# Two mixers and two expert layers on one core: decay gates moved to ScalarE, gate features projected earlier, output weights converted further ahead, and the first expert query put ahead of two weight conversions

## The chip, the cores and the metric

One core of a Trainium2 chip runs the whole program. The metric is device time in microseconds (us) of one execution. The engines are TensorE (PE, its weight loads PEld), VectorE (DVE), ScalarE (ACT), GpSimd (POOL) and the queue engine SyncE (SP).

## The reference

`x` is 256 tokens by 1024 features, all in fp32. Two blocks follow one another:

```
x = x + mixer1(rmsnorm(x)) ; x = x + peer(rmsnorm(x)) ; x = rmsnorm(x)      # first block
x = x + mixer2(rmsnorm(x)) ; x = x + peer(rmsnorm(x)) ; x = rmsnorm(x)      # second block
```

`peer` picks, for each token and each of 8 heads, 16 of 16,384 single-neuron experts from two sets of 128 keys, gathers their two rows of 1024 numbers, and sums gate * gelu(u.x) * v.

`mixer2` projects its input to ten groups of 1024 features. Three go through a causal convolution of width 4 and silu and become q, k, v of a gated delta rule in chunks of 64: q and k are brought to unit length, a triangular system (I + tril(k k^T beta decay)) is solved per chunk, with decay = exp(G_i - G_j) below the diagonal and G the running sum of the log gates g. The output is normed and gated by silu(ag). A second recurrence takes f (forget gates, `bf`), q (`bq`), input (`bi`) and an output gate (`bg`). The two results go through `w_branch_a` and `w_branch_b`, are weighted with sigmoid(ga) and sigmoid(gb), summed, and go through `w_out`.

## The kernel before, in words

All activations stay on chip. The program has five instruction streams, each written by a function of its own (`tensor_program`, `scalar_program`, `vector_program`, `gpsimd_program`, `sync_program`), and every order is written out by hand. Semaphores join them: `full(key)` says that TensorE has filled a PSUM bank, `taken(key)` that the bank was read and is free. TensorE takes the eight banks in turn.

**Weights.** `plan` lists all weight blocks in the order of use. SyncE loads each block (512 KB) into one of four slots of `ring`. Most blocks are cut into two pieces. A piece is converted into `parts` (6 places): ScalarE writes the high part (`hi`, a rounding copy, line 903) and VectorE or GpSimd the low part (`lo` = raw - hi, lines 1283 and 2134). `by_pool(p)` says which of the two does piece p. TensorE then makes three matrix products for one exact one (`mm3`, lines 357 to 359). An item of four pieces gives 256 output columns and costs 48 matmuls. ScalarE's conversion of piece p waits until TensorE has used piece p - 6. `ahead(n)` in each stream means: let the conversions go n pieces further, to six beyond the present position, but never beyond `cap[0]`. `w_branch_a` (`wa`) is used raw from the ring, in whole blocks; `cap` holds conversions back behind its blocks (`behind_wa`).

**Mixer 2** (about 842 to 1349 us of the span), stages in order of TensorE:
1. 12 convolution items (`conv`). VectorE runs the taps and silu of each; ScalarE its tanh. Between them `delta_gates` makes the gates: VectorE fills `TG` (16 slices, triu scaled by g, line 1796), TensorE sums them over rows into four banks `D` (line 662), VectorE takes the gaps to G and clips them into `DT` (line 1802), ScalarE takes exp, VectorE masks with `triu` (`decay`, line 1807).
2. `ag` item 0, transposes of q, k, v to tokens (`qk`, line 677), `ag` items 1 to 3. Meanwhile VectorE makes the unit lengths (squares, sums, root on ScalarE, products: lines 1858 to 1873; call it the unit chain). Then q, k, v are transposed back (`back`, line 688).
3. Products `L` and `Q` (line 705) times `DT`, and a block inverse in 24 steps (`inverse_y`, line 732, `inverse_xt`, line 741, `inverse_turned`, line 697).
4. The state products, then the second recurrence with 7 levels (`level_ex`, `level_exp`, `level_qk`, `level_taken`; TensorE line 819), one item between two levels.
5. Tail: `features("wb")`, `ya` 2 and 3, `yb` 0 to 3, `w_out2`, residual `x3`.

The items `bf`, `bq`, `bi`, `ya` 0 and 1, `bg`, `ga`, `gb`, `ya` 2 and 3 (`fillers`) are put between the other stages one by one with `item()`, in the same order in every stream.

**Expert layers** (`experts(e, ...)`, e = 1 and 2): GpSimd loads `keys` (line 2146), TensorE makes query item 0, `keyed(0)` scores it against the keys (line 581), ScalarE moves the scores to `S` (line 1034), VectorE `chosen(0)` picks the first 16 experts of each token (lines 1556 to 1606), and GpSimd starts 256 indirect loads of 128 rows of 8 KB each (line 2156, ten landing places). For each loaded set VectorE makes the dot product (line 1630), ScalarE the weight (line 1053), TensorE the sum (line 604). The choices of the later heads and query items 3 to 7 are fitted in between.

The arena's regions are reused by hand: `BF` lies over the first columns of `CT`, which holds q, k, v by feature until the state products.

Of the kernel before, what the change touches and what calls it, by code (L numbers as in the profile page):

```python
# [25 lines left out]
NLEV = 7  # L26

# [51 lines left out]
def build(nc, d, out):  # L79
    ctx = ExitStack()  # L80
    with ctx:
# [142 lines left out]
        BF = region(2048, 2048, c=8)  # L224
# [11 lines left out]
        SS = region(26624, 1024, h=8)  # L236
        WT = region(27648, 1024, h=8)
# [3 lines left out]
        bkf, bff, bqf = region(10240, 2048), region(2048, 2048), region(4096, 2048)  # L241
        BB, BFs, bb = spare[:, :].rearrange("p (s n) -> p s n", s=16), region(2048, 2048, s=16), spare[:, :]
# [88 lines left out]
        def tensor_program(pq, pe):  # L331
# [307 lines left out]
            def delta_gates():  # L639
# [16 lines left out]
                yield  # L656
                yield
                yield
                for q in range(4):
                    o = bank(("D", q))  # L660
                    pq.wait_ge(*on(("TG", 15)))
                    pe.matmul(o[:, :], ones, TG[:, 4 * q:4 * q + 4, :], start=True, stop=True).then_inc(*full(("D", q)))
                    yield
# [45 lines left out]
            def items():  # L709
                for name, i in fillers:  # L710
                    if name in ("bf", "bq"):
                        yield by_feature, (name, i), "w_in2", "n1"
                    elif name == "ya":
                        yield by_token_whole, (name, i), "wa", "oT", oT
                    else:
                        yield by_token, (name, i), "w_in2", "n1"
            left = items()

            def item():
                kind, *a = next(left)  # L720
                kind(*a)

# [170 lines left out]
        def scalar_program(aq, ac):  # L893
# [229 lines left out]
            def delta_gates():  # L1123
# [1185 lines left out]
```

## Time and profile before

| | |
|---|---|
| median of 3 runs | 2039.79 us (2035.16 to 2040.49) |
| profiled execution | 2036.71 us, span 2034.9 us |
| mean granted TensorE clock | 0.973 |
| PE / PEld / DVE / ACT / POOL busy | 84% / 51% / 66% / 45% / 41% |
| HBM read | 635.07 MB, 313 GB/s over the span |

The profile shows one execution. "Idle before, with a releaser" is the time in which an engine waited, and the instruction of another engine or DMA whose end let it go on. The busy share of TensorE is modelled from pipelined instructions, so it says little alone; its waits say more.

### The profile page before, as it was taken

The numbers are of one execution on the slowest core, as the hardware profiler recorded it, in microseconds if no ns is written. First come the engines' busy times: TensorE is split into PE (matmuls) and PEld (weight loads), VectorE is DVE, ScalarE is ACT, GpSimd is POOL, SyncE is SP. The second block draws the span as 40 slices with busy tenths as digits, with TensorE's granted clock in tenths as the row PEclk, the third lists the DMA queues.
The fourth block names the chain that finished last, engine by engine and source line by source line (L and its number), as shares of the span: only waits on it lengthen the run. The fifth ranks groups of instructions, "written<-read, shape, count | busy, mean of one in ns | idle before, by whom it ended". The sixth has DMA issues, their size and how long they took to land.

```text
span 2034.9 us, 22626 instructions
## 1 busy us (share of the span) xinstructions
PE 1702.4 (84%) x7622; PEld 1047.5 (51%) x7622; DVE 1336.4 (66%) x2922; ACT 913.9 (45%) x2366; POOL 839.4 (41%) x762
## 2 busy tenths in 40 slices
PE   8986889877887778789799989977899787777887
PEld 7985444422322222579799989973444222222222
DVE  4666776766776664499646773547776677667644
ACT  5554545444544443445324344454444444444443
POOL 4325333333333333367525465544333333333331
PEclk9998999999999999999899999989999999999999
DMA  7446999999999999543213333559999999999996
GB/s 247 129 129 267 420 421 421 422 421 421 422 421 421 421 421 422 216 135 125 73 53 101 100 112 114 167 169 421 421 421 421 421 422 422 421 422 421 421 422 286
DMA packets 102052, 637.60 MB, mean 313 GB/s; under 512 B 11264, under 2 KB 12544, under 8 KB 36144
## 3 DMA queue, kind: packets, MB, share of 16 engines
q0 software_dynamic: 75216, 543.73, 64.3%
q1 hardware_dynamic: 26720, 92.43, 14.1%
q8 instruction: 60, 0.98, 0.2%
q14 instruction: 56, 0.46, 0.1%
HBM read 635.07 MB, written 1.05 MB: 313 GB/s over the span
## 4 chain that ended last, share of the span: by engine, by line
PE 38%; DMA 34%; DVE 16%; ACT 8%; issue 3%; POOL 0%; SPq 0%; DVEq 0%; ACTq 0%
DMA arena<-in_uv,arena 29%; PE pb L604 19%; DMA spare<-in_uv,arena 4%; PE pb L357 4%; PE pb L358 4%; PE pb L359 4%; ACT arena L1053 3%; DVE arena L1630 3%; PE pb L430 1%; PE pb L741 1%; ACT parts L903 1%; PE pb L732 1%; DVE arena L1821 1%; DVE parts L1283 1%; DMA arena<-in_sk 1%
## 5 line engine op out<-in xcount | busy, mean ns | idle before, releaser
L604 PE MATMUL pb<-arena 128*128 128x512 f32 x1848 | 910.2, 622 | 223.9 <-ACT arena L1053 222.0
L1630 DVE SCALAR_TENSOR_TENSOR arena<-arena,pb 128x1024 f32<-128x1024 f32 x462 | 563.3, 1219 | 375.2 <-DMA arena<-in_uv,arena 375.2
L2156 POOL DMA_INDIRECT arena<-in_uv,arena x462 | 438.3, 949 | 734.0 <-PE pb L604 681.9
L604 PEld LDWEIGHTS pb<-arena 128*128 128x128 f32 x1848 | 321.8, 192 | 779.3 <-ACT arena L1053 511.3
L2134 POOL TENSOR_TENSOR parts<-ring,parts 128x512 fp32r<-128x512 f32 x228 | 340.1, 1510 | 346.3 <-ACT parts L903 344.0
L1045 ACT ACTIVATE arena<-arena 128x1 f32<-128x1 f32 x512 | 103.3, 202 | 621.7 <-DVE arena L1630 567.3
L903 ACT ACTIVATE parts<-ring 128x512 fp32r<-128x512 f32 x328 | 197.8, 627 | 198.8 <-PE pb L359 183.2
L1053 ACT ACTIVATE arena<-cst,arena 128x128 f32<-128x128 f32 x512 | 205.5, 401 | 48.7 <-ACT arena L1048 1.1
L357 PE MATMUL pb<-xl,parts 128*128 128x256 f32 x704 | 221.6, 315 | 4.1 <-DVE xl L1315 2.6
L358 PE MATMUL pb<-xh,parts 128*128 128x256 f32 x704 | 201.3, 286 | 0.0
L359 PE MATMUL pb<-xh,parts 128*128 128x256 f32 x704 | 201.1, 286 | 0.0
L357 PE MATMUL pb<-parts,xh 128*128 128x256 f32 x608 | 176.7, 291 | 14.2 <-DVE parts L1283 9.6
L358 PE MATMUL pb<-parts,xl 128*128 128x256 f32 x608 | 174.2, 287 | 0.0
L359 PE MATMUL pb<-parts,xh 128*128 128x256 f32 x608 | 174.1, 286 | 0.0
L1048 ACT ACTIVATE arena<-arena 128x1 f32<-128x1 f32 x512 | 150.8, 294 | 19.3 <-ACT arena L1045 0.4
L1283 DVE TENSOR_TENSOR parts<-ring,parts 128x512 fp32r<-128x512 f32 x100 | 78.2, 791 | 104.3 <-ACT parts L903 104.1
L357 PEld LDWEIGHTS pb<-xl,parts 128*128 128x128 f32 x704 | 137.2, 195 | 16.4 <-issue 13.8
L358 PEld LDWEIGHTS pb<-xh,parts 128*128 128x128 f32 x704 | 137.3, 195 | 10.8 <-issue 10.8
L359 PEld LDWEIGHTS pb<-xh,parts 128*128 128x128 f32 x704 | 136.9, 195 | 0.0
L357 PEld LDWEIGHTS pb<-parts,xh 128*128 128x128 f32 x608 | 118.9, 196 | 15.1 <-DVE parts L1283 10.0
L358 PEld LDWEIGHTS pb<-parts,xl 128*128 128x128 f32 x608 | 119.0, 196 | 0.0
L604 PE MATMUL pb<-spare,arena 128*128 128x512 f32 x200 | 99.6, 621 | 23.2 <-ACT arena L1053 23.1
(297 smaller groups left out, 1779.2 us busy)
## 6 DMA issues: line engine op xcount, KB each, us to landing
ring<-in_w_in SPq DMA_DIRECT2D x108, 512.0 KB, 3.5
ring<-in_wq SPq DMA_DIRECT2D x32, 512.0 KB, 6.1
ring<-in_w_out SPq DMA_DIRECT2D x16, 512.0 KB, 3.6
arena<-in_uv,arena POOLq DMA_INDIRECT x462
ring<-in_wa SPq DMA_DIRECT2D x8, 512.0 KB, 3.4
ring<-in_wb SPq DMA_DIRECT2D x8, 512.0 KB, 3.8
arena<-in_sk POOLq DMA_DIRECT2D x2, 1024.0 KB, 6.3
arena<-in_tail POOLq DMA_DIRECT2D x1, 1280.0 KB, 11.3
```

Of the source, the lines that this page charges most:

```text
L357: pe.matmul(o, lh, rl, start=start, stop=False, skip_group_check=True)
L358: pe.matmul(o, ll, rh, start=False, stop=False, skip_group_check=True)
L359: return pe.matmul(o, lh, rh, start=False, stop=stop, skip_group_check=True)
L604: ins = pe.matmul(ys[hf][:, :], diags[:, k % 4, :], lands[k % LANDS][:, D + hf * 512:D + (hf + 1) * 512], start=k % (8 * K) == 0, stop=k % ...
L903: ac.activation(split(p)[0], raw(p), ACT.Copy).then_inc(*up("a_hi", ("hi", p)))
L1045: ac.activation(acted[:, k:k + 1], hidden[:, k:k + 1], ACT.Gelu).then_inc(*up("a_gelu", ("gelu", e, k)))
L1048: ac.activation(weight_of[:, k:k + 1], acted[:, k:k + 1], ACT.Copy, scale=gate[:, k:k + 1]).then_inc(*up("a_weight", ("weight", e, k)))
L1053: ac.activation(diags[:, k % 4, :], ident, ACT.Copy, scale=weight_of[:, k:k + 1]).then_inc(*up("a_diag", ("diag", e, k)))
L1283: ve.tensor_tensor(lo, raw(p), hi.bitcast(F32), ALU.subtract).then_inc(*up("v_lo", ("lo", p)))
L1630: ve.scalar_tensor_tensor(z, z, 1.0, xg[t], ALU.mult, ALU.mult, accum_out=hidden[:, k:k + 1]).then_inc(*up("v_dot", ("dot", e, k)))
L2134: gp.tensor_tensor(lo, raw(p), hi.bitcast(F32), ALU.subtract).then_inc(*up("g_lo", ("lo", p)))
L2156: gp.indirect_dma_start(lands[k % LANDS], None, rows_uv, bass.IndirectOffsetOnAxis(ap=eidx[:, k:k + 1], axis=0)).then_inc(*up(f"dma_rows{k ...
```

## The change

- `delta_gates`: ScalarE writes the 16 slices of `TG` (four per step), and TensorE makes the four `D` banks after `ag` item 1. ScalarE makes `DT` in `decay_gaps` as relu(G - D), 4 activations per bank, and its exp has scale -1. VectorE masks `DT` after the `back` copies.
- `EARLY = 2`: `bf` 0 and 1 are projected between `ag` 3 and `back`. In the block inverse one item (at step 7) stays where three stood. For this `BF`, `EX[0]` move to 26624, `SS`, `WT` to 28672, and `KW[1]` to 2048. The small bounds `lb` are made between taps 10 and 11.
- ScalarE makes `root("unit")` after it has copied `ag` 2; its copies of the first inverse stay behind `ag_tanh`, which no longer waits for `lb`.
- `cap` has four stages: at each `ya` item the conversions may go another four pieces or up to the next `wa`.
- `by_pool`: GpSimd makes all low parts of `w_in2` up to block 67 (before: up to 63).
- `yb` item 3: VectorE makes the low features of `w_out2` 0 and 1 before its products with `yb` 3.
- `experts`: VectorE does `chosen(0)` before `with_gain(0)`, and puts only 6 instead of 8 pieces ahead of it (12 in all, as before). GpSimd starts the keys' load after two pieces fewer, in both layers.

```diff
+EARLY = 2
-        BF = region(2048, 2048, c=8)
+        BF = region(26624, 2048, c=8)
-        SS = region(26624, 1024, h=8)
-        WT = region(27648, 1024, h=8)
+        SS = region(28672, 1024, h=8)
+        WT = region(29696, 1024, h=8)
-        EX = [region(2048, 2048), region(30720, 2048)]
+        EX = [region(26624, 2048), region(30720, 2048)]
-        KW = [region(20480, 2048), region(26624, 2048)]
+        KW = [region(20480, 2048), region(2048, 2048)]
-            if name == "w_in2" and i >= 64:
+            if name == "w_in2" and i >= 68:
...
             for i in range(1, 4):
                 by_token(("ag", i), "w_in2", "n1")
+                if i == 1:
+                    for q in range(4):
+                        o = bank(("D", q))
+                        pq.wait_ge(*on(("TG", 15)))
+                        pe.matmul(o[:, :], ones, TG[:, 4 * q:4 * q + 4, :], start=True, stop=True).then_inc(*full(("D", q)))
+            for _ in range(EARLY):
+                item()
             for c2 in range(12):
...
             for n, (lev, g) in enumerate(steps):
-                if (4 * lev + g) % 8 == 7:
+                if n == 7:
                     item()
...
+                if key[0] == "ya":
+                    cap[0] = (behind_wa[0] + 4, behind_wa[1], behind_wa[1] + 4, len(pieces))[key[1]]
+                ahead(0 if key[0] == "ya" else 4)
...
+                for s in range(16):
+                    ac.activation(TG[:, s, :], triu, ACT.Copy, scale=sv["g"][:, s:s + 1]).then_inc(*up("a_delta", ("TG", s)))
+                    if s % 4 == 3:
+                        yield
+            def decay_gaps(qs):
+                for q in qs:
+                    aq.wait_ge(*full(("D", q)))
+                    for s in range(4 * q, 4 * q + 4):
+                        ins = ac.activation(DT[:, s, :], pb[place["D", q]][:, (s % 4) * P:(s % 4 + 1) * P], ACT.Relu,
+                                            bias=sv["G"][:, s:s + 1], scale=-1.0)
+                    ins.then_inc(*taken(("D", q)))
...
             copy(AG[:, :, T:2 * T], half(("ag", 1)), ("ag", 1))
+            decay_gaps((0, 1))
+            ahead(4)
+            decay_gaps((2, 3))
+            copy(AG[:, :, 2 * T:3 * T], half(("ag", 2)), ("ag", 2))
             root(nrm, "unit")
-            for i in range(2, 4):
-                ahead(4)
-                copy(AG[:, :, i * T:(i + 1) * T], half(("ag", i)), ("ag", i))
+            for q in range(4):
+                aq.wait_ge(*on(("taken", ("D", q))))
+            ac.activation(DT, DT, ACT.Exp, scale=-1.0).then_inc(*up("a_delta", "D_exp"))
+            ahead(4)
+            copy(AG[:, :, 3 * T:4 * T], half(("ag", 3)), ("ag", 3))
+            for _ in range(EARLY):
+                item()
...
                 vq.wait_ge(*on((tag, "rs")))
-                ahead(8)
-                with_gain(0)
+                ahead(12 - PARTS)
                 for _ in chosen(0):
                     pass
+                with_gain(0)
                 gates(0)
-                ahead(4)
+                ahead(PARTS)
...
+            vq.wait_ge(*on("D_exp"))
+            ve.tensor_tensor(DT, DT, bm(triu, 16), ALU.mult).then_inc(*up("v_delta", "decay"))
             vq.wait_ge(*on("decay"))
...
                 vq.wait_ge(*full(key))
+                if i == 3:
+                    features_lo("w_out2", lambda c: ones[:, 0:1], (0, 1))
                 ve.tensor_tensor(z, half(key), z, ALU.mult).then_inc(*taken(key))
...
-            ahead(18 * 4)
+            ahead(18 * 4 - PARTS + 4)
...
-                ahead(8)
+                ahead(PARTS - 4 + 8)
                 ahead(8 * 4 - PARTS - 8)
...
+            for _ in range(EARLY + 1):
+                item()
+            for q in range(4):
+                silu(q)
+            for _ in range(len(fillers) - EARLY - 1):
+                item()
+            ahead(8 * 4 - PARTS + 4)
             experts(2, "w_out2", d["sk2"], d["ffn2"], d["fin2"], d["uv2"])
```

## Rows read from the trace of the kernel before

**Rows 1.** Stretches: busy us (instructions) per engine, granted clock, DMA share, GB/s.
```profile
180.50:842.00 661.50, 536.34 (x1327) 216.77 (x1326) 447.75 (x1115) 297.58 (x883) 243.22 (x256) 0.98 1.00 413
842.00:1369.00 527.00, 477.14 (x3801) 466.71 (x3802) 344.53 (x501) 226.86 (x396) 289.79 (x195) 0.96 0.37 116
1369.00:2034.90 665.90, 535.07 (x1311) 214.43 (x1310) 444.18 (x1102) 295.92 (x876) 242.19 (x256) 0.98 0.99 409
```

**Rows 2.** TensorE's waits, 840 to 1400 us: total, times, longest.
```profile
PE pb L357 <- DVE parts L1283: 9.6, 2, 5.7
PE pb L688 <- DVE arena L1873: 9.3, 1, 9.3
PE pb L662 <- DVE arena L1796: 7.4, 1, 7.4
...
PE pb L357 <- DVE xl L1315: 3.6, 2, 3.1
PE pb L732 <- ACT arena L914: 2.6, 1, 2.6
PE pb L677 <- ACT arena L914: 2.6, 1, 2.6
PE pb L581 <- DMA arena<-in_sk: 2.1, 1, 2.1
```

**Rows 3.** Timeline of TensorE around the D banks: start, us, instruction, [idle before].
```profile
894.86 2.08 PE L662 MATMUL pb<-arena,cst 128*128 128x512 f32 x2 [7.37 <-DVE arena L1796]
...
903.28 1.02 PE L662 MATMUL pb<-arena,cst 128*128 128x512 f32 x2
...
909.89 1.02 PE L662 MATMUL pb<-arena,cst 128*128 128x512 f32 x2
```

**Rows 4.** VectorE by line and shape, 869 to 947 us: busy us, mean ns.
```profile
L1796 DVE TENSOR_SCALAR arena<-cst,small 128x128 f32<-128x128 f32 x16 | 9.5, 664 | 0.0
...
L1802 DVE TENSOR_SCALAR arena<-pb,small 128x128 f32<-128x128 f32 x16 | 4.5, 338 | 0.0
...
L1807 DVE TENSOR_TENSOR arena<-arena,cst 128x2048 f32<-128x2048 f32 x1 | 2.3, 2293 | 0.4 <-ACT arena L1145 0.4
```

**Rows 5.** Timeline of VectorE: the unit chain, and its last product's shape later.
```profile
951.01 2.28 DVE L1858 TENSOR_TENSOR arena<-arena 128x2048 f32<-128x2048 f32 x1
...
960.68 0.35 DVE L1307 RECIPROCAL small<-small 128x32 f32<-128x32 f32 x1 [0.30 <-ACT small L924]
...
974.54 2.28 DVE L1873 TENSOR_TENSOR arena<-arena,small 128x1024 f32<-128x1024 f32 x1
...
1073.32 1.22 DVE L1959 TENSOR_TENSOR arena<-arena,small 128x1024 f32<-128x1024 f32 x1
```

**Rows 6.** Timeline of GpSimd: low parts beside the taps and beside the unit chain.
```profile
882.24 5.14 POOL L2134 TENSOR_TENSOR parts<-ring,parts 128x512 fp32r<-128x512 f32 x4 [1.59 <-ACT parts L903]
...
961.25 17.93 POOL L2134 TENSOR_TENSOR parts<-ring,parts 128x512 fp32r<-128x512 f32 x8 [1.00 <-ACT parts L903]
```

**Rows 7.** Timeline of ScalarE: scaled 128x128 copies; exp and conversions at level 5.
```profile
846.61 0.62 ACT L1108 ACTIVATE xh<-pb,cols 128x128 fp32r<-128x128 f32 x2
...
1204.50 1.91 ACT L1250 ACTIVATE arena<-arena 128x2048 f32<-128x2048 f32 x1 [4.17 <-DVE arena L2055]
1206.32 2.17 ACT L903 ACTIVATE parts<-ring 128x512 fp32r<-128x512 f32 x4
```

**Rows 8.** Timelines at the start of expert layer 1: all engines.
```profile
155.87 0.76 POOL L2146 DMA_DIRECT2D arena<-in_sk  x1
...
162.09 1.16 PE L581 MATMUL pb<-arena 128*128 128x128 f32 x8 [1.96 <-DMA arena<-in_sk]
...
163.35 0.84 ACT L1034 ACTIVATE arena<-pb,small 128x256 f32<-128x256 f32 x2 [2.06 <-PE pb L581]
...
168.78 0.69 DVE L1283 TENSOR_TENSOR parts<-ring,parts 128x512 fp32r<-128x512 f32 x1 [10.40 <-ACT parts L903]
...
172.13 0.48 DVE L1556 MAX8 arena<-arena 128x8 f32<-128x128 f32 x2
...
180.49 1.53 POOL L2156 DMA_INDIRECT arena<-in_uv,arena  x1 [12.33 <-DVE arena L1606]
```

**Rows 9.** Timelines at the start of expert layer 2.
```profile
1351.28 0.84 ACT L1034 ACTIVATE arena<-pb,small 128x256 f32<-128x256 f32 x2 [3.15 <-PE pb L581]
...
1360.68 0.48 DVE L1556 MAX8 arena<-arena 128x8 f32<-128x128 f32 x2
...
1369.04 1.52 POOL L2156 DMA_INDIRECT arena<-in_uv,arena  x1 [12.32 <-DVE arena L1606]
```

More of the change, by code:

```diff
@@ L655, in delta_gates, with items, item @@
                 pe.matmul(o[:, 16:32], ones, sv["g"], start=True, stop=True).then_inc(*full("G"))
[L656 to L663, printed above, removed]
+            def items():
+                for name, i in fillers:
+                    if name in ("bf", "bq"):
+                        yield by_feature, (name, i), "w_in2", "n1"
+                    elif name == "ya":
+                        yield by_token_whole, (name, i), "wa", "oT", oT
+                    else:
+                        yield by_token, (name, i), "w_in2", "n1"
+            left = items()
+            def item():
+                kind, *a = next(left)
+                kind(*a)
             gate_steps = delta_gates()
@@ L1140, in delta_gates @@
                 yield
-                yield
-                for _ in range(4):
-                    yield
-                aq.wait_ge(*on(("taken", ("D", 3))))
-                ac.activation(DT, DT, ACT.Exp).then_inc(*up("a_delta", "D_exp"))
+                for s in range(16):
[9 more added lines that the diff above has]
+                    ins.then_inc(*taken(("D", q)))
             def conv_tanh(i):
@@ L1875, in vector_program @@
-            at["unit"] = on(("unit_vb", 1))
-            ahead(8)
-            for c2 in range(1, 12, 2):
-                copy(CT[:, 2 * c2:2 * c2 + 2, :], half(("back", c2)), ("back", c2))
-            vq.wait_ge(*on("decay"))
-            for g in range(4):
-                vq.wait_ge(*full(("L", g)))
-                ve.tensor_tensor(LT[:, g], bank4(("L", g)), DTg[:, g], ALU.mult).then_inc(*taken(("L", g)))
-                vq.wait_ge(*full(("Q", g)))
-                ve.tensor_tensor(AQ[:, g], bank4(("Q", g)), DTg[:, g], ALU.mult).then_inc(*taken(("Q", g)))
-                vq.wait_ge(*on(("taken", ("L", g))))
-                ve.copy_predicated(LT[:, g], bm(ident.bitcast(U32), 4), bm(ones, 4)).then_inc(*up("v_inverse", ("M", g)))
-                vq.wait_ge(*on(("M", g)))
-                ve.tensor_tensor(XT[:, g], LT[:, g], bm(signs[0], 4), ALU.mult).then_inc(*up("v_inverse", ("XT", 0, g)))
@@ L1933, in item @@
                 waiting.append(key)
+            for _ in gate_steps:
+                pass
+            ahead(4)
+            for n, (g, t) in enumerate((g, t) for g in range(6) for t in range(NT)):
+                if n % 2:
+                    copy(QK[:, t, 4 * g:4 * g + 4, :], bank4(("qk", g, t)), ("qk", g, t))
+            ahead(4)
+            for t in range(NT):
+                sq = region(6144 + 2048 * t, 2048, c=16)
+                for g in range(4):
+                    vq.wait_ge(*on(("taken", ("qk", g, t))))
+                ve.tensor_tensor(sq, QK[:, t, 0:16, :], QK[:, t, 0:16, :], ALU.mult).then_inc(*up("v_unit", ("unit_sq", t)))
+                vq.wait_ge(*on(("unit_sq", t)))
+                ve.tensor_reduce(nrm[:, 16 * t:16 * t + 16], sq, AX, ALU.add).then_inc(*up("v_unit", ("unit_ss", t)))
@@ new lines, in vector_program @@
+            at["unit"] = on(("unit_vb", 1))
+            ahead(8)
+            for _ in range(EARLY):
+                item()
+            for c2 in range(1, 12, 2):
+                copy(CT[:, 2 * c2:2 * c2 + 2, :], half(("back", c2)), ("back", c2))
+            vq.wait_ge(*on("D_exp"))
+            ve.tensor_tensor(DT, DT, bm(triu, 16), ALU.mult).then_inc(*up("v_delta", "decay"))
+            vq.wait_ge(*on("decay"))
+            for g in range(4):
+                vq.wait_ge(*full(("L", g)))
+                ve.tensor_tensor(LT[:, g], bank4(("L", g)), DTg[:, g], ALU.mult).then_inc(*taken(("L", g)))
+                vq.wait_ge(*full(("Q", g)))
+                ve.tensor_tensor(AQ[:, g], bank4(("Q", g)), DTg[:, g], ALU.mult).then_inc(*taken(("Q", g)))
+                vq.wait_ge(*on(("taken", ("L", g))))
+                ve.copy_predicated(LT[:, g], bm(ident.bitcast(U32), 4), bm(ones, 4)).then_inc(*up("v_inverse", ("M", g)))
+                vq.wait_ge(*on(("M", g)))
+                ve.tensor_tensor(XT[:, g], LT[:, g], bm(signs[0], 4), ALU.mult).then_inc(*up("v_inverse", ("XT", 0, g)))
```

143 lines of the change are left out of this document (45 added, 98 removed).

## The prediction

> **What bounds the kernel now.** I first cut the span into stretches. In the two gather stretches the DMA engines are busy for 1.00 and 0.99 of the time at 413 and 409 GB/s [rows 1]: they carry a fixed number of bytes, so each ends a fixed time after its first indirect load. Only what comes before that first load can move their end. The middle stretch, 527 us of mixer 2 and the start of the second expert layer, has a DMA share of 0.37; TensorE is busy for 477 us of it [rows 1]. So I then read TensorE's waits there. Two large single ones belong to stages that the change touches: 7.4 us for `TG` and 9.3 us for the unit chain; the others that it may touch are 2.6, 2.6, 9.6 in two, 3.6 in two and 2.1 us [rows 2]. Last I read the timelines at the start of both expert layers: VectorE stands idle for 10.40 us behind a low part that waits for ScalarE's high part (and that for query 1 on TensorE), while the scores that `chosen(0)` needs are ready [rows 8].
>
> **Expert starts (both layers).** The scores of head 0 are in `S` at 163.35 + 0.84 = 164.2, but `chosen(0)` starts at 172.13 [rows 8]: 7.9 us go to two low parts (pieces 12 and 13 of the queries) and `with_gain`. With 6 instead of 8 pieces ahead, all of them are GpSimd's and VectorE has none before `chosen(0)`. The low parts, `with_gain` and `gates` come behind the choice, where the first rows are still on their way. On top, GpSimd issues the keys' load at 155.87 behind two low parts that wait for TensorE, and TensorE waits 1.96 us for it [rows 8], 2.1 us in layer 2 [rows 2]. The load now goes out when the last piece of the output weights is done, about 10 us sooner, and is covered. Some 0.6 us of the wait stays, for the query's own eviction, so 1.4. Layer 1: 7.9 + 1.4 = 9.3 us. Layer 2: scores at 1351.28 + 0.84 = 1352.1, choice at 1360.68 [rows 9], 8.6 + 1.5 = 10.1, and up to 0.9 more if `keyed(0)` runs at the short time of layer 1; I take 10.5. From the choice to the first indirect load it stays 8.4 us in both [rows 8, 9]. Against it: weight block 10 of the queries is loaded behind the moved low parts, so its 512 KB now fall into the saturated stretch: 0.524 MB / 420 GB/s = 1.25 us each. Net 8.0 and 9.3. Bounds: nothing, if later choices or the eleventh load are what paces the start; 11 us each. I take the full shift, because DVE, ACT and PE after the first row are ordered as before.
>
> **D banks.** The step with the wait runs from the end of the item before (887.5) to 903.28; a step without it takes 909.89 - 903.28 = 6.6 us [rows 3]. 15.8 - 6.6 = 9.2: 7.4 of wait, 1.8 because TensorE then worked at a lowered clock (the pair takes 2.08 for 1.02). VectorE loses 9.5 + 4.5 + 2.3 us of work here [rows 4], without which it just keeps up with the items of 5.9 us; the four D products move, they don't vanish. ScalarE gets 16 + 16 operations on 128x128. Its own nearest row gives 0.31 us each [rows 7], the dearest is VectorE's `TG` slice beside GpSimd with 0.66 [rows 4]: 10 to 21 us in all. I take the first, since it is the same engine and shape. Per convolution item ScalarE has four conversions (2.2 us [rows 7]) and a tanh, 3 of 5.9 us, so 1.3 us more for four slices are hidden; uncovered, `TG` would cost TensorE 5 us. I take 9.2. VectorE, 13 us earlier at the end of silu 11, also softens the 2.6 us wait for the `qk` copies, but the `lb` operations (1 us) and VectorE's share of the copies stand there: I take 2.4, bounds 0 and 2.6. Together 11.6.
>
> **Unit chain and early items.** TensorE waits 9.3 us for the chain; 2 x 5.9 us of `bf` now stand there. Two things eat from it. First, the root now stands on ScalarE behind the copy of `ag` 2 and four `decay_gaps`: the reciprocal that waits 0.30 us today [rows 5] would wait until TensorE has done `ag` 1, four D products and `ag` 2. By my order of events the mean is ready 9.4 us after the chain's start and the root some 8.5 us later. The rest of the chain, from the reciprocal at 960.68 to 976.82, is 16 us [rows 5], so the chain is late by 8.5 and ends 3 us after TensorE would be done with `bf` 1. Second, in this stretch a low part takes 17.93 / 8 = 2.24 us against 5.14 / 4 = 1.29 beside the taps [rows 6], while an item wants four in 5.9 us. The pieces of `bf` 0's second half are converted only after the root and the exp of `DT`, so about six low parts stand on the path at 2.24 for TensorE's 1.47: with the release of the first, 5.7 us of TensorE's time are lost. The two losses overlap, the larger counts. 9.3 - 5.7 = 3.6 us gain. Bounds: 9.3, if GpSimd keeps up; and -1, if both losses add.
> A row beside it: the 1024-wide product takes 2.28 us while GpSimd works and 1.22 alone [rows 5]. The Trainium skill (SBUF — State Buffer, "SBUF: two separate sides") says that a VectorE operation with two SBUF inputs and a GpSimd operation hold their shared ports in turn, each for its whole duration. By that rule a low part costs its own time plus VectorE's, 1.29 + 1.22 = 2.5 us for 2.24 measured; the loss would be 1.6 us larger and the sum 1.6 us less.
>
> **Behind it.** The mask of `DT` (2.3 us [rows 4]) now stands between the `back` copies and the first `L` product on VectorE; it is covered by TensorE's eight `L` and `Q` products and by the item behind them, and would cost 2.3 if they were gone. `ag_tanh` no longer waits for `lb`, so ScalarE is free for the first inverse copies: of the 2.6 us wait for line 732 I take 2.4. The 24 inverse steps had no wait in levels without an item, so taking two items out costs nothing: TensorE paces them. Cover gone, a step would wait for VectorE's eviction.
>
> **Levels and tail.** The 9.6 us for VectorE's low parts are 5.7 in `ga` 0 and 3.9 in `gb` 0 [rows 2]. The former isn't VectorE's fault: the high parts start at 1206.32, behind `ends_exp` [rows 7]. On GpSimd the low part costs 1.3 instead of 0.7, so +0.7. Letting four `bg` pieces go at `ya` 0 takes GpSimd off VectorE's ports while it makes level 3's inputs: -1.4. `gb` 0 is untouched. Net 0.7 gain; bounds -2 and +4. At `yb` 3 the wait of 3.1 us (in the 3.6 [rows 2]) loses the product and sum of VectorE that stand first, but still waits for ScalarE's high features: 1.1 gain, bounds 0 and 1.8. The cap at `ya` 2 changes nothing: ScalarE there waits for the loads of `wb`.
>
> **Sum.** 8.0 + 11.6 + 3.6 + 2.4 + 0.7 + 1.1 + 9.3 = 36.7 us. The profiled execution took 2036.71 (span 2034.9), so 2000.0; the median of the runs is 3.1 above it, and I put the new time at 2003 in the same terms.
>
> **Rivals.**
> (a) VectorE and GpSimd take turns through the whole unit chain, so that each low part costs 1.29 + 1.22 = 2.5 us, and the loss adds to that of the late root instead of overlapping it: -1 for +3.6, and 2.4 and 2 us more where the same turns reach the silus and the `qk` copies. 36.7 - 9 = 28, 2012 us; the expert starts come in full. For: 2.24 us per low part [rows 6]. Against: while the chain waits for the root, GpSimd has the ports to itself.
> That they take turns is what the page named above states; the time is worked out from the rows.
> (b) The expert starts do not carry over: the saturated stretch ends with the last choice or with block loads, each start gives 3 us for 8.7. 36.7 - 11 = 25, 2014 us, and with (a) 2023. Against: 0.99 and 1.00 of DMA.
> (c) More comes back: VectorE without its low part contention closes `ga` 0, the early items hide the whole unit chain: 36.7 + 5.7 + 4 = 46, 1993 us.
> (d) The change doesn't do what it says: TensorE's waits move one for one (the inverse now meets an unfinished mask, the root eats the early items) and the early first load is lost to a late second choice. Of the 36.7 then go 17.3 at the starts and 17.6 in the middle: 1.8 stay, 2038 us.
> (e) Slower: ScalarE, with 32 more operations and in-order conversions behind waits, starves TensorE. They stand beside seven items, each with 2.9 us free, 20 us. It decides from (20 + 37) / 32 = 1.8 us per operation on, where the rows show 0.31 to 0.66 [rows 4, 7]; with 2 us each it is 2047.
>
> **Chances.** Forecast (36.7 within about 5) 0.55, (a) 0.15, (b) 0.10, (c) 0.13, (d) 0.04, (e) 0.03. I take the range from (c) to (a) with (b): 1990 to 2018. 0.3% (6 us) is about what a measurement of this kernel can tell from no change: faster 0.93, same 0.04, slower 0.03.
>
> **What would show it.** The first indirect load of layer 1 at about 171 instead of 180.5, VectorE's 10.4 us wait before it gone, no TensorE wait for the keys. No wait at line 662; the reciprocal of the unit chain waiting about 8 us for the root; several waits of 1 to 2 us for line 2134 in `bf` 0 and 1, and none above 3 at line 688. The first inverse step some 18 us nearer to the layer's start, counted with the two items done. A wait of some 6 us still in `ga` 0, now for GpSimd. The prediction is wrong if the gather stretch gets longer than 661 + 2 us, or if ScalarE's 128x128 operations are far above 0.3 us.

## The result and the profile after

The changed kernel takes 2007.38 us (median of four runs, 2005.91 to 2009.00) against 2038.34 us before (2035.16 to 2040.49): ratio 0.985, 95% interval 0.9832 to 0.9867. That is 31.0 us faster; the forecast was 2003, 35 us. The profiled execution took 2005.91 us, its span is 2004.1 us, against 2036.71 and 2034.9 us before.

First the three stretches of the changed kernel, cut as in [rows 1] at the first indirect load of each layer (columns as there):

```profile
171.10:833.00 661.90, 539.02 (x1342) 219.17 (x1341) 449.64 (x1118) 298.67 (x885) 243.22 (x256) 0.98 1.00 413
833.00:1336.30 503.30, 470.94 (x3783) 460.48 (x3784) 332.79 (x464) 233.80 (x427) 288.41 (x197) 0.98 0.38 121
1336.30:2004.10 667.80, 540.28 (x1329) 218.02 (x1328) 446.74 (x1107) 297.22 (x879) 242.29 (x256) 0.98 0.99 409
```

The gather stretches are still saturated, at the same 413 and 409 GB/s. The middle is some 24 us shorter, and TensorE is busy in 471 of its 503 us. TensorE's waits from 840 to 1370 us (columns as in [rows 2]):

```profile
PE pb L358 <- POOL parts L2141: 9.6, 6, 4.9
PE pb L358 <- DVE parts L1299: 3.9, 1, 3.9
PE pb L684 <- ACT arena L914: 2.7, 1, 2.7
PE pb L358 <- DVE xl L1331: 2.7, 2, 2.1
PE pb L684 <- DVE arena L1310: 2.5, 1, 2.5
...
PE pb L582 <- ACT arena L914: 0.8, 1, 0.8
```

Against [rows 2], the waits of 7.4 us for `TG` and 9.3 us for the unit chain are gone, and so are those of 2.6 us for line 732 and 2.1 us for the keys. What is new: 4.7 us in five waits for GpSimd's low parts in `bf` 0 and 1 (the sixth, 4.9 us, is `ga` 0), and two more waits at the `qk` transposes (line 684, once 677): 2.5 us for VectorE's copies, and 0.5 us for its taps (not among the lines shown).

The best ruler in this study is the trace cut at fixed events. Each column is the time from one event to the next (us, good to about 0.1), read from the first and last starts of six lines: k is the first product of scores and keys in a layer, i the first indirect load, s the last gather sum, G the first product of mixer 2's gates, q the first `qk` transpose, L the first product behind `back`.

| profiled run | start to k1 | k1-i1 | i1-s1 | s1-G | G-q | q-L | L-k2 | k2-i2 | i2-s2 |
|---|---|---|---|---|---|---|---|---|---|
| before | 162.1 | 18.4 | 658.5 | 30.5 | 70.9 | 44.6 | 364.1 | 19.9 | 658.8 |
| after | 159.1 | 12.0 | 660.0 | 31.2 | 58.1 | 58.0 | 346.3 | 11.6 | 660.7 |
| after, once more | 164.1 | 11.9 | 660.2 | 31.3 | 58.1 | 58.0 | 346.3 | 11.6 | 659.9 |

The two traces of one kernel agree within 0.2 us in seven columns and within 0.8 in the last, but differ by 5.0 us up to k1. Of the 30.8 us between the spans of before and after, 3.0 stand ahead of k1; 1.2 of them are the keys' wait; the other 1.8 lie within that scatter.

Now the rows that answer to [rows 8], VectorE and GpSimd at the start of layer 1:

```profile
161.68 0.49 DVE L1572 MAX8 arena<-arena 128x8 f32<-128x128 f32 x2 [5.07 <-ACT arena L1034]
...
164.03 1.44 DVE L1585 TENSOR_TENSOR arena<-arena 128x256 f32<-128x256 f32 x1
...
170.63 0.18 DVE L1622 SCALAR_TENSOR_TENSOR arena<-arena 128x16 uint32<-128x16 f32 x1
```
```profile
162.52 2.67 POOL L2141 TENSOR_TENSOR parts<-ring,parts 128x512 fp32r<-128x512 f32 x2 [0.50 <-ACT parts L903]
171.09 1.25 POOL L2163 DMA_INDIRECT arena<-in_uv,arena  x1 [5.90 <-DVE arena L1622]
```

The choice starts as soon as the scores are there, and the first indirect load goes out at 171.09 us, as predicted. From the choice's start it takes 9.41 us, though, where [rows 8] give 8.36. In layer 2 it takes 9.46 for 8.36, and there it is another operation that is long, the cast of 32 indices:

```profile
1329.58 1.27 DVE L1588 CAST arena<-arena 128x32 f32<-128x32 uint32 x1
```
```profile
1328.08 2.73 POOL L2141 TENSOR_TENSOR parts<-ring,parts 128x512 fp32r<-128x512 f32 x2 [0.45 <-ACT parts L903]
```

The conv tail and the unit chain on VectorE, which answer to [rows 5], and GpSimd's low parts, those beside the conv tail and those of `bf`, which answer to [rows 6]:

```profile
919.08 1.26 DVE L1847 TENSOR_TENSOR small<-cols 128x8 f32<-128x8 f32 x1
...
926.78 1.24 DVE L1854 TENSOR_TENSOR small<-small 128x8 f32<-128x8 f32 x1
928.05 0.20 DVE L1856 RECIPROCAL small<-small 128x8 f32<-128x8 f32 x1
928.28 0.95 DVE L1858 TENSOR_TENSOR small<-small 128x8 f32<-128x8 f32 x1
929.27 1.19 DVE L1860 TENSOR_TENSOR small<-small 128x8 f32<-128x8 f32 x1
...
943.90 0.18 DVE L1319 TENSOR_SCALAR small<-small 128x32 f32<-128x32 f32 x1
953.92 0.35 DVE L1323 RECIPROCAL small<-small 128x32 f32<-128x32 f32 x1 [9.84 <-ACT small L924]
```
```profile
925.04 5.39 POOL L2141 TENSOR_TENSOR parts<-ring,parts 128x512 fp32r<-128x512 f32 x4 [4.73 <-ACT parts L903]
...
957.71 20.38 POOL L2141 TENSOR_TENSOR parts<-ring,parts 128x512 fp32r<-128x512 f32 x12 [6.54 <-ACT parts L903]
```

Two things are to be seen. Four of the six `lb` operations, on 8 numbers per partition, take 0.95 to 1.26 us each; with the other two (0.18 and 0.20 us) and what stands between them they are 5.1 us, and they stand ahead of VectorE's first `qk` copy. And the reciprocal waits 9.84 us for the late root.

In the kernel before, the six operations took 1.04 us in all, at a place where GpSimd was idle (for 20.66 us, up to 999.84). The first and the last of them there, and GpSimd's next row:

```profile
996.78 0.16 DVE L1890 TENSOR_TENSOR small<-cols 128x8 f32<-128x8 f32 x1
...
998.07 0.17 DVE L1900 TENSOR_TENSOR small<-small 128x8 f32<-128x8 f32 x1
```
```profile
999.84 4.95 POOL L2134 TENSOR_TENSOR parts<-ring,parts 128x512 fp32r<-128x512 f32 x4 [20.66 <-ACT parts L903]
```

### The profile page after: what moved, and what is told of

The parts are those of the page before. It is cut to its first block, busy times and chain, and to the rows that moved or that the text cites. A ratio compares the mean times of both kernels' runs of the same rounds, so it can differ in the third digit from the quotient of the medians.

```text
span 2004.1 us, 22628 instructions
## 1 busy us (share of the span) xinstructions
PE 1699.6 (85%) x7622; PEld 1042.9 (52%) x7622; DVE 1329.5 (66%) x2888; ACT 922.0 (46%) x2398; POOL 838.7 (42%) x764
## 3 DMA queue, kind: packets, MB, share of 16 engines
q1 hardware_dynamic: 26720, 92.43, 14.2%
HBM read 635.07 MB, written 1.05 MB: 317 GB/s over the span
## 4 chain that ended last, share of the span: by engine, by line
PE 37%; DMA 35%; DVE 15%; ACT 8%; issue 3%; POOL 1%; SPq 0%; DVEq 0%; ACTq 0%; POOLq 0%
DMA arena<-in_uv,arena 32%; PE pb L605 18%; PE pb L358 4%; PE pb L359 4%; PE pb L360 4%; ACT arena L1053 3%; DMA spare<-in_uv,arena 3%; DVE arena L1646 3%; PE pb L431 1%; DVE arena L1823 1%; PE pb L741 1%; DVE arena L1836 1%; PE pb L732 1%; ACT arena L1048 1%; POOL parts L2141 1%
## 5 line engine op out<-in xcount | busy, mean ns | idle before, releaser
L358 PEld LDWEIGHTS pb<-parts,xh 128*128 128x128 f32 x608 | 118.6, 195 | 13.6 <-POOL parts L2141 5.1
```

The costliest lines, as they stand in the source:

```text
L358: pe.matmul(o, lh, rl, start=start, stop=False, skip_group_check=True)
```

## The experiments

All are compared with the kernel before on the same chip; where I set one against the changed kernel, it is by the median of the latter's own runs (2007.38, and 2009.72 in the last set) and by the columns. The kernel before has medians of 2038.34, 2038.89, 2040.32 and 2037.85 us in the four sets, so a difference to 2007.38 across sets can be off by some 2 us; effects of that size are read from the columns.

**The expert starts alone.** The kernel before, with the new order in both expert layers only.

```diff
-                ahead(8)
-                with_gain(0)
+                ahead(12 - PARTS)
                 for _ in chosen(0):
                     pass
+                with_gain(0)
                 gates(0)
-                ahead(4)
+                ahead(PARTS)
...
```

> The kernel before with only the expert layers' part of the change (queries' low parts, gain and gates behind the first choice, keys loaded at once). Theory: the trace of after puts the starts at 7.6 us (layer 1) and 7.8 us (layer 2) net, so 15.4 us below before, ratio 0.992, with each first indirect load 9 to 10 us earlier and 1.5 to 2 us of that lost while the gathers run. Rival, the starts don't carry over: 3 us each, ratio 0.997. Rival, the prediction's own figure: 17.3 us, ratio 0.9915.

2024.65 us, ratio 0.9927 (0.991 to 0.9943): 14.2 us. Columns: k1-i1 11.9, i1-s1 659.9, k2-i2 11.6, i2-s2 660.5, the same as in the changed kernel. Layer 1 gives 18.4 - 11.9 = 6.5 and 1.2 of the keys' wait, less 1.4 in the gathers: 6.3. Layer 2 gives 8.3 and 1.3, less 1.7: 7.9. Together 14.2 us, as timed: the starts carry over, apart from some 1.5 us each. (The span of this one trace, 2025.3 us, holds 1.9 us more up to k1 and 2.7 more from s1 to k2, where the kernel is that of before. With one trace of each kernel I can't tell how much of the 2.7 us is scatter.)

**No item ahead of the chain.** The levels have their three items again.

```diff
-EARLY = 2
+EARLY = 0
...
-                if n == 7:
+                if n in (3, 11, 19):
```

> The changed kernel with no item ahead of the unit chain; the two items go back into the levels. Theory: the late root then sets the end of the chain (reciprocal waits some 10 us as before), the products behind it run without GpSimd and end 6 us earlier than in the changed kernel, and 11.9 us of items are still to be done: 6 us slower than the changed kernel, ratio to before 0.988. TensorE waits 11 to 12 us for the chain. Rival, the low parts cost all that the early items give: within 1 us of the changed kernel (0.985). Rival, the chain ends where it did: 12 us slower (0.991).

2018.03 us, ratio 0.9898 (0.9878 to 0.9917), 10.7 slower than the changed kernel; my 6 was too low, the rival with 12 nearly right. TensorE's row at `back`:

```profile
972.42 3.86 PE L702 MATMUL pb<-cst,arena 128*128 128x128 f32 x17 [13.21 <-DVE arena L1921]
```

With the late root and without the items TensorE waits 13.2 us, more than the 9.3 of [rows 2]. From q to L it is only 2.1 us shorter than in the changed kernel (55.9 for 58.0), for 11.9 us of items that are still to come. From the end of the `qk` transposes to `back`, the D products taken off, this kernel is 3.9 us slower than the kernel before, just as 13.2 us of wait for 9.3, and the changed kernel is 4.0 faster (below). So the early items give 7.9 us there; nearly all the rest of the 10.7 is 1.9 in the `back` transposes, which take 7.3 us for 5.4 behind the long wait, and 0.7 in the levels. The 3.9 us are what the root's new place costs when nothing covers it; that it is the root alone is argued, but moving it gives back 3.8 in the changed kernel (below).

**The `lb` operations elsewhere.** The changed kernel; the two groups of operations stand in the gather loop of layer 1, the exponential too.

```diff
+                    if e == 1 and k == 40:
+                        vq.wait_ge(*on("ld_cols"))
+                        ve.tensor_tensor(lbc, c_lb[:, 0, :], c_lb[:, 1, :], ALU.max).then_inc(*up("v_lb", "lb_max"))
...
+                    if e == 1 and k == 60:
+                        vq.wait_ge(*on("lb_exps"))
+                        ve.tensor_tensor(oml, p2[:, 0, :], p2[:, 1, :], ALU.add).then_inc(*up("v_lb", "lb_sum"))
...
```

> The changed kernel with the six small lb operations and their exponential in layer 1's gather stretch instead of around the last taps of the convolutions. Theory: 5.1 us of VectorE time leave the way to the qk copies; TensorE's waits there, 0.5 + 2.7 + 2.5 us, fall to 1.5 to 2 in all: 4 us faster than the changed kernel, ratio to before 0.983. Rival: ScalarE's four conversions ahead of its copies (the 2.7 us wait) take over: 1 us faster. Rival: the small operations only filled idle time: nothing.

2002.92 us, ratio 0.9822 (0.9806 to 0.9838): 4.5 faster than the changed kernel. q-L is 51.9 for 58.0 us. What is left of the waits at the transposes:

```profile
929.50 2.45 PE L684 MATMUL pb<-cst,arena 128*128 128x128 f32 x20 [1.93 <-ACT arena L914]
```

One wait of 1.9 us stands for three of 0.5, 2.7 and 2.5. That is 3.7 us less; the rest of the 6.1 goes with the clock. The last twelve transposes of the changed kernel take 2.82 us at a granted clock of 0.50, these last twenty 2.45 us at 1.00. The windows of both kernels, the same 20 us around the transposes:

```profile
921.10:941.10 20.00, 14.36 (x96) 12.73 (x95) 19.23 (x24) 9.35 (x19) 10.06 (x7) 0.83 0.28 85
```
```profile
924.90:944.90 20.00, 18.07 (x134) 15.84 (x133) 17.12 (x19) 12.45 (x27) 14.75 (x10) 1.00 0.45 132
```

Behind the longer waits TensorE's granted clock is 0.83 in the mean (full speed for part of the time and half of it, 1.2 instead of 2.4 GHz, for the rest), behind the one short wait it stays at 1.00.

**The slices twice.** The changed kernel; ScalarE makes each `TG` slice a second time, into unused memory.

```diff
+                    ac.activation(spare[:, s * P:(s + 1) * P], triu, ACT.Copy, scale=sv["g"][:, s:s + 1])
                     ac.activation(TG[:, s, :], triu, ACT.Copy, scale=sv["g"][:, s:s + 1]).then_inc(*up("a_delta", ("TG", s)))
```

> The changed kernel with every one of the sixteen gate slices made twice on ScalarE (a second 128x128 copy each into unused memory). Theory: ScalarE is busy for some 4.1 of the 5.9 us of a convolution item, 1.3 us more per item are hidden: no new TensorE wait there, span unchanged within 0.5 us at that stage. Rival, ScalarE is near its limit: conversions come late and TensorE waits up to 5 us for high parts in items 4 to 8.

G-q is 58.1 us as in the changed kernel. The window of the slices, in which ScalarE is busy for 17.66 us (the fourth busy time) for 13.41 in the changed kernel:

```profile
883.90:903.90 20.00, 20.00 (x169) 20.00 (x169) 19.86 (x36) 17.66 (x45) 20.00 (x15) 1.00 0.60 184
```

TensorE, VectorE and GpSimd are busy throughout. ScalarE could carry twice the slices; the rival (e) is wrong. (This single run took 2011.6 us; the 1.4 and 1.2 us more from q to L and from L to k2 come behind the edit, where the granted clock was 0.74 in the transposes' window instead of 0.83. I can't say whether the edit has a part in that.)

**The root earlier.** The changed kernel, with ScalarE's root between the decay gaps.

```diff
             decay_gaps((0, 1))
+            root(nrm, "unit")
             ahead(4)
             decay_gaps((2, 3))
             copy(AG[:, :, 2 * T:3 * T], half(("ag", 2)), ("ag", 2))
-            root(nrm, "unit")
```

> The changed kernel with ScalarE's root of the unit norms directly behind the first two decay gaps instead of behind all four and the copy of ag 2. Theory: the reciprocal waits 2 to 3 us instead of 9.8 and the chain ends 7 us earlier; what then holds TensorE are the low parts of bf 0 (4.7 us in five waits today), whose high parts start up to 2 us sooner since the root is already done, and GpSimd has the ports to itself sooner: 2 to 4 us faster than the changed kernel, ratio to before 0.983 to 0.984. Rival, the larger of two losses counts and the low parts are it: within 0.5 us. Rival, ScalarE's conversions for ag 2 and ag 3 come late behind the root: 1 to 2 us slower.

2004.56 us, ratio 0.9825 (0.9809 to 0.9842): 2.8 faster than the changed kernel. The reciprocal, and TensorE's waits for low parts up to `back`:

```profile
947.28 0.35 DVE L1323 RECIPROCAL small<-small 128x32 f32<-128x32 f32 x1 [0.66 <-ACT small L924]
```
```profile
PE pb L358 <- POOL parts L2141: 1.3, 3, 0.5
```

The wait of 9.8 us is 0.7, and of it TensorE gets 3.8 (q-L 54.2 for 58.0). Most of this is the low parts' 4.7 us, now 1.3.

**GpSimd's work out of the choice.** The changed kernel; GpSimd takes six of the queries' first pieces instead of eight, VectorE the other two behind the choice.

```diff
-                return 4 <= p - first_piece[name] < 12
+                return 4 <= p - first_piece[name] < 10
...
-                ahead(12 - PARTS)
+                ahead(10 - PARTS)
                 for _ in chosen(0):
                     pass
+                ahead(2)
...
```

> The changed kernel with the last two of GpSimd's eight low parts of the queries given to VectorE, directly behind the first choice, so that GpSimd's work ends sooner under the choice. Theory: scores to first indirect load take 9.5 to 9.9 us in the changed kernel and 8.4 with GpSimd still; with the last 2.7 us of GpSimd's work gone some 1 us comes back in each layer, 2 us in all, ratio to before 0.984. Rival: the scores of query 1, now later, make VectorE and so the gathers wait, 0 to 2 us slower. Rival: the choice is slow for another reason, no change of the first load.

2007.95 us, ratio 0.9843 (0.9825 to 0.9861): no difference from the changed kernel. VectorE and GpSimd at the same place of layer 1:

```profile
168.19 0.40 DVE L1585 TENSOR_TENSOR arena<-arena 128x256 f32<-128x256 f32 x1
```
```profile
174.20 1.18 POOL L2164 DMA_INDIRECT arena<-in_uv,arena  x1 [8.02 <-DVE arena L1622]
```

The step came out as expected: the sum on line 1585 takes 0.40 us for 1.44 (and the cast in layer 2 0.18 for 1.27), k1-i1 is 10.9 for 12.0, k2-i2 10.6 for 11.6. But i1-s1 grows from 660.0 to 660.8, and i2-s2 is 660.7, at the top of the changed kernel's 659.9 to 660.7. Of 2.1 us at the first loads some 1 is left at the last sums, too little to measure. The windows of the 5 us ahead of each first indirect load, for the changed kernel and for this one, show what happened to the rest:

```profile
166.10:171.10 5.00, 5.00 (x44) 5.00 (x43) 4.76 (x16) 4.36 (x8) 0.01 (x1) 1.00 0.36 105
```
```profile
169.20:174.20 5.00, 3.86 (x33) 3.66 (x31) 4.76 (x16) 4.02 (x8) 0.00 (x1) 1.00 0.01 6
```

105 for 6 GB/s over 5 us are 0.50 MB, the size of one weight block. SyncE's issues show the block: in the changed kernel it goes out 6.1 us after k1, ahead of the first rows. Here none goes out then, and four instead of three follow close behind the first rows. The low parts that free its place come later here; that this is the reason is read from the program's order.

**Two late edits undone.** Blocks 64 to 67 of `w_in2` shared between GpSimd and VectorE again, and the features of `w_out2` behind `yb` 3 instead of in it.

```diff
-            if name == "w_in2" and i >= 68:
+            if name == "w_in2" and i >= 64:
...
-                if i == 3:
-                    features_lo("w_out2", lambda c: ones[:, 0:1], (0, 1))
...
+            features_lo("w_out2", lambda c: ones[:, 0:1], (0, 1))
```

> The changed kernel with two small edits of the late stages undone: the pieces of blocks 64 to 67 of w_in2 shared between GpSimd and VectorE again, and the first two high-and-low feature groups of w_out2 behind the last gate instead of in it. Theory: TensorE's wait in ga 0 stays as large (4.9 now, 5.7 in the kernel before, because the high parts start late), the wait before w_out2 goes from 2.1 back to 3.1: 1 to 2 us slower in that stretch. Rival: neither changes.

TensorE's waits from 1150 to 1320 us:

```profile
PE pb L358 <- DVE parts L1299: 8.3, 2, 4.5
PE pb L358 <- DVE xl L1331: 3.1, 1, 3.1
```

This is a single run, 2009.62 us, so the waits have to tell. The one before `w_out2` is 3.1 again for 2.1: that edit is worth 1.0. In `ga` 0 it is 3.8 for VectorE instead of 4.9 for GpSimd: giving all these pieces to GpSimd cost 1.1 us. The 4.5 is `gb` 0, 3.9 in the changed kernel; four other variants that leave it alone have 4.5 too. L-k2 is 346.9 for 346.3.

**Slices and gaps on VectorE, TensorE's order new.** The changed kernel; VectorE makes the `TG` slices between the taps as before the change, and the decay gaps behind `mean`.

```diff
+                for s in range(16):
+                    ve.tensor_scalar(TG[:, s, :], triu, sv["g"][:, s:s + 1], None, ALU.mult).then_inc(*up("v_delta", ("TG", s)))
...
             mean("unit", nrm, 1.0)
+            for q in range(4):
+                vq.wait_ge(*full(("D", q)))
+                for s in range(4 * q, 4 * q + 4):
+                    ins = ve.tensor_scalar(DT[:, s, :], pb[place["D", q]][:, (s % 4) * P:(s % 4 + 1) * P], sv["G"][:, s:s + 1],
+                                           0.0, ALU.subtract, ALU.min)
...
```

> The changed kernel with the gate slices and the decay gaps on VectorE again, TensorE's order as changed: the D products still come behind ag 1, the slices between the taps as before the change, the gaps in VectorE's idle time behind the mean. Theory: VectorE has no idle time between the taps, so its 9.5 us of slices come back as TensorE waits at the conv items and the qk transposes, 8 to 10 us slower than the changed kernel, ratio to before 0.989; the gaps cost nothing, they fit into the 9.8 us wait for the root. Rival: TensorE's order alone gave the gain (no wait for the last slice at the D products), within 1 us of the changed kernel.

2014.00 us, ratio 0.9881 (0.9866 to 0.9896), 4.3 slower than the changed kernel beside it. G-q is 64.3 for 58.1 us. VectorE's slices, the first small operation of `lb`, and the gaps; then GpSimd's next row, and TensorE's in the items:

```profile
877.00 3.76 DVE L1806 TENSOR_SCALAR arena<-cst,small 128x128 f32<-128x128 f32 x8
...
884.86 5.84 DVE L1806 TENSOR_SCALAR arena<-cst,small 128x128 f32<-128x128 f32 x8
...
929.04 0.15 DVE L1846 TENSOR_TENSOR small<-cols 128x8 f32<-128x8 f32 x1
...
952.99 4.22 DVE L1913 TENSOR_SCALAR arena<-pb,small 128x128 f32<-128x128 f32 x16
961.15 0.35 DVE L1317 RECIPROCAL small<-small 128x32 f32<-128x32 f32 x1 [3.94 <-ACT small L924]
```
```profile
933.90 5.39 POOL L2146 TENSOR_TENSOR parts<-ring,parts 128x512 fp32r<-128x512 f32 x4 [5.33 <-ACT parts L903]
```
```profile
896.41 0.58 PE L358 MATMUL pb<-xl,parts 128*128 128x256 f32 x1 [3.85 <-POOL parts L2146]
```

The 9.6 us of slices put 6.2 us on the way to q. Part of it is then absorbed in the wait for the root (3.94 for 9.84 us), so 4 us are left at k2 (497.7 from s1 for 493.8). My 8 to 10 left that cover out. The gaps stand in the same wait and cost nothing.

**Two combinations.** The first: `lb` elsewhere, the root earlier, the exponential of `DT` one item later, and the queries' two pieces on VectorE. The second: `lb` elsewhere, the root earlier, blocks 64 to 67 shared. The one edit that isn't above, in ScalarE's order:

```diff
+            ahead(4)
+            copy(AG[:, :, 3 * T:4 * T], half(("ag", 3)), ("ag", 3))
+            item()
             for q in range(4):
                 aq.wait_ge(*on(("taken", ("D", q))))
             ac.activation(DT, DT, ACT.Exp, scale=-1.0).then_inc(*up("a_delta", "D_exp"))
-            ahead(4)
-            copy(AG[:, :, 3 * T:4 * T], half(("ag", 3)), ("ag", 3))
-            for _ in range(EARLY):
-                item()
+            item()
```

> The changed kernel with four edits: the lb operations in the gather stretch, the root behind the first two decay gaps, the exponential of the decay behind the first early item's conversions, and the last two low parts of the queries on VectorE behind the choice. Theory: 4.5 (measured alone) + 3 + 2 = 9 to 10 us below the changed kernel, ratio to before 0.980. Rival, the middle edits compete (with the lb operations gone the chain is early enough): 6 us, 0.982. Rival, the later exponential holds the mask and the inverse: 4 us.

1998.08 us, ratio 0.9796 (0.9781 to 0.9812). From s1 to k2 483.9 us, 9.7 less than the changed kernel: 6.3 (`lb`) and 3.0 (root) add up to 9.3, and the 0.4 that are left are too little to credit the later exponential with. The second is run beside the changed kernel, once more:

> The changed kernel once more, unchanged, on the chip of the two runs beside it, as their yardstick. Theory: ratio to before 0.985 within 0.002. In the stages that the edits don't touch its trace should repeat the first one; only the time up to the first keyed product may differ, by up to 4 us, as it does between the runs so far (159.1 to 163.4 us).

2009.72 us, ratio 0.9859 (0.9844 to 0.9875).

> The changed kernel with the lb operations in the gather stretch, the root behind the first two decay gaps, and the low parts of blocks 64 to 67 shared with VectorE again. Theory, from the three traces: 6.3 + 3.0 + 1.1 = 10 us below the changed kernel, ratio to before 0.980, with no choice edit and the exponential left where it was, since neither showed anything. Rival: the shared low parts lose in this company (VectorE is later in ga 0), 9 us. Rival: one of the two edits left out did carry something: 7 us.

1996.49 us, ratio 0.9793 (0.978 to 0.9806), beside 2009.72 for the changed kernel: 13.2 us faster by the medians, 10.8 by the columns from s1 to k2 (483.0 for 493.8). It has the lowest median here, but the first combination can't be told from it: the intervals of their ratios overlap nearly in full, and from s1 to k2 they are 0.9 us apart. Its middle stretch:

```profile
837.80:1330.50 492.70, 468.58 (x3784) 459.07 (x3785) 332.17 (x459) 233.46 (x425) 290.22 (x196) 0.98 0.40 123
```

TensorE is busy for 469 of 493 us.

## Why the prediction came out right, and where it was off

The time lies in the range, on the right side, 4 us above the forecast. By the sum's own terms, in the columns and the timelines:

| term | predicted | trace | what is behind it |
|---|---|---|---|
| expert start, layer 1 | 8.0 | 6.1 | 6.4 to the first load, 1.2 keys, -1.5 in the gathers |
| D banks | 9.2 | 9.1 | G-q 12.7 less the 3.6 us of D products, which moved |
| softened `qk` wait | 2.4 | -3.6 | transposes with waits 13.6 for 10.0 us |
| unit chain, early items | 3.6 | 4.0 | end of transposes to `back`, items and D products taken off |
| `back` | 0 | 1.7 | 5.4 for 7.1 us, clock |
| inverse copies of X | 2.4 | 2.5 | no wait at line 732 |
| s1 to G | 0 | -0.7 | granted clock 0.71 for 0.83 in the first 10 us |
| levels, tail | 1.8 | 2.2 | what is left of s1 to k2: `ga` 0, `w_out2` |
| expert start, layer 2 | 9.3 | 7.7 | 8.3 and 1.3 keys, -1.9 in the gathers |
| up to k1 | 0 | 1.8 | scatter, 159.1 to 164.1 us in twelve traces with the new starts |
| sum | 36.7 | 30.8 | |

The `qk` row is 6.0 us off, all of the shortfall. The rest cancels, and that is luck: 3.5 less at the starts, 3.5 more from two rows that the sum had at nothing, the clock at `back` and the scatter up to k1.

**The step that failed** is "VectorE, 13 us earlier at the end of silu 11, also softens the 2.6 us wait for the `qk` copies, but the `lb` operations (1 us) ... stand there: I take 2.4". The bounds, 0 and 2.6, had no loss in them. Two things were wrong. VectorE is not 13 us earlier relative to TensorE: when TensorE no longer waits for `TG`, both get there earlier, and VectorE, with no idle time between 870 and 925 us, is as far behind as before: silu 11 ends 5.7 us after the first `qk` transpose in the kernel before, and 6.4 after it in the changed one. And the `lb` operations take 5.1 us instead of 1. Moving them alone gave 6.1 us of trace in this stage and 4.5 of time.

Why they are so long is seen by comparing rows. The 1 us is right for the place that they had, beside an idle GpSimd. The 128x8 maximum takes 1.26 us in the changed kernel, 0.16 in the kernel before, and 0.15 in the one with VectorE's slices, at 929.04, where GpSimd is idle for 5.33 us up to 933.90; the reciprocal of the same size, with one input, takes 0.20. A low part of GpSimd takes 1.3 us [rows 6]. The four long operations end at 920.34, 928.01, 929.24 and 930.46 us, each 0.02 to 0.03 us after one of GpSimd's low parts (920.31, 927.99, 929.21, 930.43). So each takes what is left of the low part that it meets. The Trainium skill states this (SBUF — State Buffer, "SBUF: two separate sides"): the pair is held for a whole instruction and the loser fully blocks; here the trace agrees, with 0.95 to 1.26 us per operation. I had used that rule for the 1024-wide products and not for the small ones, for which it matters most.

**The D banks** came out to 0.1 us. The experiment splits them: with the slices on VectorE and the new order G-q is 64.3, 6.2 more than on ScalarE. So the slices' place gives 6.2; the other 2.9 are TensorE's order together with the gaps and the mask, which no longer stand between the taps, and these were not told apart. The slices on ScalarE take 1.27 us per four, as taken from [rows 7].

**The unit chain** was predicted by its parts, and they hold: the reciprocal waits 9.8 us (about 8 predicted), TensorE waits 4.7 us for low parts (5.7), there is no large wait at `back`. The low parts take 20.38 / 12 = 1.70 us, not 2.24: the chain's products on VectorE are over at 968.0 us, halfway through them. "The larger counts" was too simple: with the root early the low parts' waits fall too, from 4.7 to 1.3. Two things differ there, counted from the first `qk` transpose. ScalarE's conversions behind the exponential start 1.5 us sooner (35.1 for 36.6), as the root (0.23 us) and its table load (1.28 us) no longer stand ahead of them; and the chain ends 8.1 us sooner (39.5 for 47.5). Which of the two gives how much was not tried.

**The starts.** The first load came at 171.09 us for "about 171"; part of this is the earlier k1. From k1 it is 12.0, where the sum's 7.9 would make 18.4 - 7.9 = 10.5. "From the choice to the first indirect load it stays 8.4 us" was wrong by 1.05 us in each layer: the choice now runs beside GpSimd's last low parts, and one of its operations waits for one: the larger sum in layer 1 (1.44 us for 0.41), the cast in layer 2 (1.27 for 0.17). The experiment took that back (10.9) and gained nothing measurable. The gathers grew by 1.5 and 1.9 us where I had 1.25 each for the weight block (1.7 and 1.2 in the second trace), so rival (b) holds for about a fifth of each start and no more. The variant whose first load is 1 us sooner still shows the mechanism a second time: 0.50 MB less ahead of the first load, and a stretch 0.8 us longer behind it. What is not loaded ahead of the first rows is loaded among them.

**The rivals.** (a) did not come: the turns cost 4.7 us, not more, and don't add to the root. (c) asked for a closed `ga` 0; it kept 4.9 us. (d) and (e) are refuted by the columns and by the doubled slices. The small terms of the levels hold with their signs: +1.1 lost by GpSimd's pieces (0.7 predicted), 1.9 gained between the kernel before and the one with the pieces shared (5.7 to 3.8; 1.4 predicted for the pieces let go, which were not tried alone), 1.0 by the features at `yb` 3 (1.1).

## What to carry to other kernels

Relief for one engine is not slack against another: when the wait of the engine that leads goes, both move, and what was hidden behind the wait stands open again. Of an edit that moves small operations, ask beside whom they now run; on VectorE with GpSimd at work six operations on 8 or 16 numbers took 5.1 us, nearly an item of TensorE, and 1.0 with GpSimd idle. And cut every trace at the same events: here seven of the columns repeat to 0.2 us where the whole run scatters by 3 to 5, so that edits of 1 us can be told.

## What the runs showed of the hardware

What a low part of GpSimd adds to a VectorE operation doesn't depend on the operation's size: up to 1.1 us for 128x8 (0.15 to 1.26) and 1.0 for 128x256 (0.40 to 1.44). It isn't only operations of two inputs: the cast of 32 indices, with one, takes 1.27 us instead of 0.17 in the ten traces in which GpSimd's last low part lies beside it, and ends 0.03 to 0.04 us after that part. The maxima and index searches of the choice kept their times beside GpSimd (0.48 to 0.49 us, 0.28 to 0.29).

Waits of 2 to 3 us cost TensorE more than their length. The transposes behind three waits of 0.5, 2.7 and 2.5 us had a mean granted clock of 0.83, and taking 3.7 us of wait away gave 6.1. Behind the 9.3 us wait before `back` the 48 transposes took 7.1 us at a mean granted clock of 0.75; in the changed kernel, at 1.00, 5.4. The windows of 20 us around them, of the kernel before (most of the wait lies in it) and of the changed kernel:

```profile
969.00:989.00 20.00, 11.16 (x84) 10.98 (x85) 14.56 (x14) 4.87 (x7) 10.18 (x5) 0.74 0.25 79
```
```profile
961.10:981.10 20.00, 16.08 (x132) 15.30 (x133) 17.76 (x14) 9.85 (x15) 16.99 (x11) 1.00 0.51 158
```

The time up to the first keyed product differs by up to 5 us between runs of the same instructions (159.1 and 164.1 us). Its cause stays open.
